# Decays of a gated delta rule read from rows spread over partitions, and formed one head pair ahead

## The reference

```python
g_f = -jnp.exp(a_log[0])[:, None] * jax.nn.softplus(a_f + dt_bias[0][:, None])
...
gc = jnp.cumsum(g.astype(f32).reshape(bn, h, n, c), axis=-1)
incl = jnp.tril(jnp.ones((c, c), dtype=bool))
strict = jnp.tril(jnp.ones((c, c), dtype=bool), -1)
decay = jnp.exp(jnp.where(incl, gc[..., :, None] - gc[..., None, :], -jnp.inf))
k_beta = k * beta
m = jnp.where(strict, jnp.einsum('bhnik,bhnjk->bhnij', k_beta, k) * decay, 0.0)
t_inv = lax.linalg.triangular_solve(eye + m, jnp.broadcast_to(eye, m.shape),
                                    left_side=True, lower=True, unit_diagonal=True)
...
intra = jnp.einsum('bhnik,bhnjk->bhnij', q, k) * decay
...
def step(s, inp):
    a_n, u_n, w_n, qd_n, kd_n, gt_n = inp
    v_new = u_n - w_n @ s
    o_n = qd_n @ s + a_n @ v_new
    s = s * gt_n + jnp.einsum('bhck,bhcv->bhkv', kd_n, v_new)
    return s, o_n
```

## Time and profile before

| | |
|---|---|
| three runs, us | 845.85, 846.38, 852.87 |
| profiled execution, us | 845.52, of it span 843.9 |
| PE busy, us | 754.1 |
| DVE busy, us | 578.0 |
| ACT busy, us | 418.9 |
| POOL busy, us | 202.4 |
| DMA moved, MB | 203.10 |
| PE granted clock over the span | 0.982 of full |
| pairs 0, 1, 2, 3 begin at, us | 90.28, 185.88, 284.76, 383.39 |

### The profile page before, as it was taken

One profiled execution on the slowest core, in us unless ns is written; L12 is line 12 of the kernel. 1 busy time (PEld: TensorE's weight loads), 2 busy tenths in 40 slices (PEclk: granted clock), 3 DMA queues, 4 the chain that ended last, 5 costly groups with the idle time before them and its releaser, 6 DMA issues.

```text
span 843.9 us, 15762 instructions
## 1 busy us (share of the span) xinstructions
PE 754.1 (89%) x6268; PEld 625.6 (74%) x6268; DVE 578.0 (68%) x861; ACT 418.9 (50%) x741; POOL 202.4 (24%) x362
## 2 busy tenths in 40 slices
PE   3998998899979998899669899989999999999974
PEld 1678887889879897799659788887777777687531
DVE  2488587768877688776876448578877775786153
ACT  3476563458434573438524335546565665573101
POOL 3102252203702344013700120011432223212201
PEclk9999999999999999999979999999999999999998
DMA  9966464666527654569866238853999999999992
GB/s 314 298 202 165 112 160 105 189 175 164 144 59 216 182 138 113 148 178 276 263 162 196 62 131 288 333 200 120 333 387 419 407 421 421 416 421 371 419 419 98
DMA packets 164678, 203.10 MB, mean 241 GB/s; under 512 B 33381, under 2 KB 137998, under 8 KB 151674
## 3 DMA queue, kind: packets, MB, share of 16 engines
q1 hardware_dynamic: 162489, 198.02, 69.4%
q0 software_dynamic: 2112, 4.04, 1.3%
HBM read 187.49 MB, written 18.10 MB: 244 GB/s over the span
## 4 chain that ended last, share of the span: by engine, by line
PE 63%; DVE 19%; DMA 10%; issue 3%; ACT 3%; POOL 1%; SPq 1%; POOLq 0%; DVEq 0%; ACTq 0%
PE bank L2558 61%; DMA raw<-in_w_e_dram 5%; DVE chan L1833 3%; DVE half_lo L1737 3%; DVE w_lo L2243 2%; PE bank L2561 2%; DMA raw<-in_w_ada_dram 1%; DMA half_raw<-in_w_out_dram 1%; SPq L622 1%; DVE lane L1913 1%; DVE lane L1942 1%; ACT w_hi L1601 1%; DMA gate_b<-dense 1%; DVE ada_sum L2063 1%; DVE ada_sum L2061 1%
## 5 line engine op out<-in xcount | busy, mean ns | idle before, releaser
L2558 PE MATMUL bank<-hT,half_hi 128*128 128x256 f32 (+1 forms) x1024 | 229.5, 319 | 10.5 <-DVE half_lo L1737 6.3
L2558 PEld LDWEIGHTS bank<-hT,half_hi 128*128 128x128 f32 x1024 | 167.5, 193 | 23.9 <-issue 9.0
L2558 PE MATMUL bank<-hT,half_lo 128*128 128x256 f32 (+1 forms) x512 | 159.9, 312 | 0.0
L1737 DVE TENSOR_TENSOR half_lo<-half_raw,half_hi 128x1024 fp32r<-128x1024 f32 x88 | 108.1, 1230 | 31.4 <-ACT half_hi L1178 30.6
L2243 DVE TENSOR_TENSOR w_lo<-raw,w_hi 128x2048 fp32r<-128x2048 f32 x36 | 88.3, 2462 | 46.5 <-ACT w_hi L1601 46.4
L2558 PE MATMUL bank<-lane 64*64 64x64 f32 (+3 forms) x1968 | 85.4, 229 | 28.3 <-DVE lane L1894 8.2
L1178 ACT CAST half_hi<-half_raw 128x1024 fp32r<-128x1024 f32 x88 | 92.0, 1048 | 32.5 <-DMA half_raw<-in_w_proj_a_dram 12.1
L2558 PEld LDWEIGHTS bank<-lane 64*64 64x64 f32 (+3 forms) x1968 | 76.5, 139 | 38.3 <-issue 21.4
L2558 PEld LDWEIGHTS bank<-hT,half_lo 128*128 128x128 f32 x512 | 98.8, 193 | 5.2
L1601 ACT CAST w_hi<-raw 128x2048 fp32r<-128x2048 f32 x36 | 68.7, 1908 | 34.2 <-PE bank L2558 18.5
L1833 DVE SCALAR_TENSOR_TENSOR chan<-bank,conv_col,chan 128x508 f32<-128x508 f32 (+3 forms) x96 | 63.2, 658 | 10.3 <-ACT chan L1249 7.7
(11 more groups left out here) (392 smaller groups left out, 1385.8 us busy)
## 6 DMA issues: line engine op xcount, KB each, us to landing
raw<-in_w_e_dram SPq DMA_DIRECT2D x96, 1024.0 KB, 10.7
half_raw<-in_w_in_dram SPq DMA_DIRECT2D x64, 512.0 KB, 4.8
half_raw<-in_w_ada_dram SPq DMA_DIRECT2D x32, 512.0 KB, 4.7
raw<-in_w_ada_dram SPq DMA_DIRECT2D x8, 1024.0 KB, 10.9
dense<-staged SPq DMA_DIRECT2D x32, 128.0 KB, 4.6
half_raw<-in_w_proj_a_dram SPq DMA_DIRECT2D x8, 512.0 KB, 5.6
half_raw<-in_w_proj_b_dram SPq DMA_DIRECT2D x8, 512.0 KB, 3.7
half_raw<-in_w_out_dram SPq DMA_DIRECT2D x8, 512.0 KB, 6.8
```

The costliest lines, as they stand in the source:

```text
L1737: dve.tensor_tensor(half_lo[m % HBUF][:, :], half_raw[n % HRING][:, :], half_hi[m % HBUF][:, :].bitcast(F32), ALU.subtract).then_inc(s["ha ...
L2558: return nc.tensor.matmul(dst, lhsT, rhs, start=start, stop=stop)
```

## The change

The cumulated decays of all heads are formed once, in `gate_totals`, as 64 rows of 128 tokens, one for each tile, head and direction. SP writes them to DRAM (`store_cum`) and reads those of one pair back, each row spread over all 128 partitions, into parts 12 to 15 of `lane` (`load_cum`, four DMAs of 256 KB). The 16 products of each pair that made the same numbers in PSUM are gone. `decay_exp` reads SBUF now and has moved: for pair 0 it stands ahead of the pairs, for pair j within the scan of pair j - 1. Freed banks let the four `scores` stand side by side in banks 4 to 7, with no wait of one for another. DVE does the four `first_level` at the start of the pair, ahead of `taps(0)`. `turn_out` waits for the `intra_mask` of the pair's tile 3, as their results share bank 7. Before, `turn_channels(0)` and `(1)` waited for `intra_mask`; now they wait for `first_level(0)` and `(1)`. The block solver on POOL and `move_inverse` on SP wait for `intra_exp` of the pair too. In `gate_sums` DVE copies the 64 rows into a `staged` buffer, and `store_cum` and `load_cum(0)` stand on SP on either side of the first `spill`. Besides, `new_value(0)` stands ahead of a cast on ACT, `ada_fold(2 * i + 1)` behind the last dense part on PE, and `ada_line_copy(2 * i + 1)` behind a copy.

```diff
         u_inv = [problems(4 + g) for g in range(4)]
-        p_blk = [problems(12 + g) for g in range(4)]
+        cum_of = [problems(12 + g) for g in range(4)]
+        p_blk = [problems(n) for n in (12, 13, 8, 9)]
 
...
 
+            def store_cum():
+                sp.wait_ge(s["gate_dve"], 4)
+                rows_of = cum_dram.rearrange("(r d n) -> r d n", d=DIRS, n=P)
+                for d in range(DIRS):
+                    load(rows_of[:, d, :], cum_rows[d * TILES * HEADS:(d + 1) * TILES * HEADS, :], s["landed_cum"])
+
+            def load_cum(p):
+                if p:
+                    sp.wait_ge(s["inverse_placed"], 4 * p)
+                else:
+                    sp.wait_ge(s["landed_cum"], 32)
+                size = 2 * DIRS * P
+                for t in range(TILES):
+                    at_ = (t * PAIRS + p) * size
+                    load(lane_part(12 + t), cum_dram[at_:at_ + size].partition_broadcast(P), s["landed_cum"])
+
             def move_rows(first, last):
...
                 spill(3 + 7 * i + 3)
+                load_cum(j)
                 after_split(DENSE_AT[3 + 7 * i + 3])
...
                 pool.wait_ge(s["m_ready"], i * TILES + TILES)
+                pool.wait_ge(s["intra_exp"], 2 * i + 2)
                 own.after(pool.memset(solved_blocks, 0.0))
...
                 act.wait_ge(s["half_used"], DENSE_AT[k] + 1)
+                if k == 2:
+                    act.wait_ge(s["landed_cum"], 32)
                 if k >= STAGES:
...
 
-            def decay_exp(g):
-                act.wait_ge(s["scores_ready"], i * 4 + (g + 1))
-                if g == 0 and i == 0:
-                    act.wait_ge(s["gate_dve"], 7)
-                cum = by_pair(bank[6 + g % 2])
+            def decay_exp(p, g):
+                if g == 0:
+                    act.wait_ge(s["landed_cum"], 32 + 64 * (p + 1))
+                    if p == 0:
+                        act.wait_ge(s["gate_dve"], 7)
                 for h in range(2):
                     for d in range(DIRS):
-                        own.mark(act.activation(p_blk[g][:, h, d, :], cum[:, h, d, :], ACT.Relu,
-                                                bias=gates[:, NEG_CUM, g, 2 * i + h, d:d + 1]))
+                        own.mark(act.activation(p_blk[g][:, h, d, :], cum_of[g][:, h, d, :], ACT.Relu,
+                                                bias=gates[:, NEG_CUM, g, 2 * p + h, d:d + 1]))
                 own.settle()
...
             def intra_exp(g):
-                cum = by_pair(bank[6 + g % 2])
+                if g == LAT:
+                    act.wait_ge(s["pair_free"], i + 1)
                 for h in range(2):
                     for d in range(DIRS):
-                        own.mark(act.activation(intra[g - LAT][:, h, d, :], cum[:, h, d, :], ACT.Relu, scale=-1.0,
+                        own.mark(act.activation(intra[g - LAT][:, h, d, :], cum_of[g][:, h, d, :], ACT.Relu, scale=-1.0,
                                                 bias=gates[:, CUM, g, 2 * i + h, d:d + 1]))
...
             ahead(DENSE_AT[2])
+            for g in range(TILES):
+                decay_exp(0, g)
             dense_copy(2)
...
                     o_scale(i - 1)
-                decay_exp(0)
+                intra_exp(2)
                 ahead(CHAN_AT[j, 0])
-                decay_exp(1)
+                intra_exp(3)
                 center(0)
...
                     o_mul(i - 1)
-                decay_exp(2)
-                decay_exp(3)
-                intra_exp(2)
                 ahead(CHAN_AT[j, 1])
                 tanh(0)
-                intra_exp(3)
                 ahead(DENSE_AT[3 + 7 * i + 0])
...
                 place_last()
+                new_value(0)
                 ahead(DENSE_AT[3 + 7 * i + 3])
-                new_value(0)
                 z_parts(0)
...
                 dense_copy(3 + 7 * i + 4)
+                decay_exp(j, 0)
+                decay_exp(j, 1)
                 state_query(2)
...
                 ahead(Z_AT[j, 1])
+                decay_exp(j, 2)
                 dense_copy(3 + 7 * i + 5)
+                decay_exp(j, 3)
                 state_query(3)
                 new_value(3)
-                ada_line_copy(2 * i + 1)
                 ahead(DENSE_AT[3 + 7 * i + 5])
                 dense_copy(3 + 7 * i + 6)
+                ada_line_copy(2 * i + 1)
                 ahead(DENSE_AT[3 + 7 * i + 6])
...
             o_scale(PAIRS - 2)
-            decay_exp(0)
-            decay_exp(1)
+            intra_exp(2)
             ahead(DENSE_AT[24])
-            decay_exp(2)
+            intra_exp(3)
             dense_copy(24)
-            decay_exp(3)
+            ahead(DENSE_AT[25])
             mix_copies()
-            ahead(DENSE_AT[25])
-            intra_exp(2)
             dense_copy(25)
-            intra_exp(3)
             dense_copy(26)
...
             def first_level(g):
+                dve.wait_ge(s["scores_ready"], i * 4 + (g + 1))
                 dve.wait_ge(s["decay_exp"], i * 4 + (g + 1))
...
                     dve.wait_ge(s["key_gates_ready"], i + 1)
-                kk = bank[4 + g % 2][:, 0:256].rearrange("p (h n) -> p h n", h=2)
+                    dve.wait_ge(s["pair_free"], i + 1)
+                kk = bank[4 + g][:, 0:256].rearrange("p (h n) -> p h n", h=2)
                 for h in range(2):
...
                 j = i + 1
-                ahead(CHAN_AT[j, 0])
                 first_level(0)
                 first_level(1)
-                taps(0)
                 first_level(2)
                 first_level(3)
+                ahead(CHAN_AT[j, 0])
+                taps(0)
                 ahead(CHAN_AT[j, 1])
...
                        gates[:, LOG_DECAY, :, :, :].rearrange("p t h d -> p (t h) d")[:, :, d])
+                for d in range(DIRS):
+                    rows_ = slice(d * TILES * HEADS, (d + 1) * TILES * HEADS)
+                    mm(bank[6][rows_, 2 * P:3 * P], gates[:, LOG_DECAY, :, :, :].rearrange("p t h d -> p (t h) d")[:, :, d],
+                       causal[:, d, :])
                 mm(bank[6][:, 64:128], ones[:, :], gates[:, LOG_DECAY, :, :, :].rearrange("p t h d -> p (t h d)"))\
...
                     pe.wait_ge(s["v_copied"], i * 2 + 2)
+                if g == LAT:
                     pe.wait_ge(s["pair_free"], i + 1)
-                if g >= 2:
-                    pe.wait_ge(s["m_ready"], i * 4 + (g - 1))
                 tok = slice(g * P, (g + 1) * P)
                 for h in range(2):
-                    mm(bank[4 + g % 2][:, h * P:(h + 1) * P], kT[i % 2][:, h, tok], kT[i % 2][:, h, tok])
+                    ins = mm(bank[4 + g][:, h * P:(h + 1) * P], kT[i % 2][:, h, tok], kT[i % 2][:, h, tok])
                     if g >= LAT:
                         q_tok = slice((g - LAT) * P, (g - LAT + 1) * P)
-                        mm(bank[4 + g % 2][:, 256 + h * P:256 + (h + 1) * P], kT[i % 2][:, h, tok], qT[i % 2][:, h, q_tok])
-                for h in range(2):
-                    for d in range(DIRS):
-                        ins = mm(by_pair(bank[6 + g % 2])[:, h, d, :],
-                                 gates[:, LOG_DECAY, g, 2 * i + h, d:d + 1].to_broadcast([P, P]), causal[:, d, :])
+                        ins = mm(bank[4 + g][:, 256 + h * P:256 + (h + 1) * P], kT[i % 2][:, h, tok], qT[i % 2][:, h, q_tok])
                 ins.then_inc(s["scores_ready"], 1)
...
                 if p < PAIRS - 1:
-                    pe.wait_ge(s["intra_exp"], p * 2 + 4)
+                    pe.wait_ge(s["intra_ready"], p * 2 + 4)
                 for h in range(2):
...
                 scores(0)
-                channels(0, 0)
                 scores(1)
-                channels(0, 1)
                 scores(2)
                 scores(3)
+                channels(0, 0)
+                channels(0, 1)
                 channels(1, 0)
...
                 solved(3)
-                ada_fold(2 * i + 1)
                 intra_sum(3)
                 dense_part(3 + 7 * i + 6, 1)
+                ada_fold(2 * i + 1)
             i = PAIRS - 1
```

20 lines of the change are left out of this document (14 added, 6 removed).

## The result

| | before | changed |
|---|---|---|
| median of the runs compared, us | 848.95 (4 runs, 845.85 to 852.87) | 863.61 (4 runs, 860.05 to 867.81) |
| profiled execution, its span | 845.52, 843.9 | 860.05, 858.4 |
| mean granted clock | 0.982 | 0.964 |
| PE busy, us | 754.1 | 752.2 |

The ratio is 1.0163, 95% interval 1.0129 to 1.0196. The forecast was 838.0, and 863.61 lies outside its range. It came out slower by over 1%, which had a chance of 0.04.

What follows compares the result with a forecast made beforehand. PE was taken to bound the kernel up to `level_p` of each pair. Terms summed to 11.45 us, less 4.5 plus 1.4 for the clock: gain 8.35, 837.2 profiled, 838.0 on the scale of the runs; range 830 to 844.

Steps and rivals of the forecast that it cites:

- that lands just in time: 0: Scans: the spread rows take 6.5 us and reach ACT when it wants them, at no cost.
- rival D: Scans: rows landing over 7 us after issue make `decay_exp` hold up `state_query(2)`; at 10.7 us, 849.1; chance 0.05.
- Numbers: Closing chances for the whole kernel: faster 0.48, within 1% 0.48, slower 0.04.
- I expect the gain to be stopped: Pairs 1 and 2: PE waits about 4.3 us at `turn_out` for `intra_mask`; removed products buy 0.1 us there.
- gains 0.1 + 2.37 = 2.45 and 0.1 + 2.01 = 2.1: Pairs 1 and 2: the inverse returns sooner, so `place_corners` no longer waits 2.37 and 2.01 us.
- -4.5 + 1.4: Granted clock: falls behind three new waits cost 4.5 us; one old fall avoided gains 1.4.
- Gain 3.5: Pair 0: PE comes 3.55 us sooner to `level_p`, where the 1.13 us wait hangs on DVE; gain 3.5.
- I take 0.3: Ahead of the pairs: added products and a DVE copy in `gate_totals` cost 0.3 us, between 0 and 1.1.
- 0.6 for pair 0 and 0.45 for pairs 1 and 2: Scans: moving `new_value(0)` ahead removes PE's 0.85 us wait, DVE late next; these gains, bounds 0 and 0.85.
- Gain 2.2: Last pair: `u_gelu` and the remainder behind it come sooner; gain 2.2 us, between 0.6 and 3.6.
- work taken from it there is time: Up to `level_p` of each pair PE works nearly without a gap, so removed work saves time until something else is late.

Runs made afterwards that it cites:

- both: Changed kernel with spread rows in their own 8 KB, loaded right behind `move_inverse`, and `intra_mask(3)` ahead of `taps(1)`: 839.58 us, ratio 0.9883.
- A quarter of the rows: Changed kernel with one spread DMA of 256 KB for each pair instead of four, other tiles' decays wrong: 848.11 us, ratio 0.9986.
- rows in a quiet place: Changed kernel with spread rows in their own 8 KB, issued right behind `move_inverse`: 852.87 us, ratio 1.0038.
- mask first: Changed kernel with `intra_mask(3)` right behind `intra_mask(2)`, ahead of `taps(1)`, in pairs 0 to 2: 849.08 us, ratio 1.0001.
- Rows of `m` first: As "both", but in pair 0 SP sends the rows of `m` ahead of the weight half: 837.86 us, ratio 0.9858.
- new value first: Kernel before the change with `new_value(0)` ahead of the cast on ACT, nothing else: 849.26 us, ratio 0.9986.

## Why the prediction was wrong

**The step that failed: "that lands just in time: 0".** The four spreads took 10.9 us in pair 1, not the 6.5 that I took. ACT then stood still for 4.68 us, and the scans lost 10.7 us where the term was 0. I had priced them by size, between a 512 KB and a 2 MB spread, and took the nearer row. Size alone does not set it. These spreads moved less than half of what weight halves moved (158 GB/s on average over 268 to 274, against 354) while the engines were just as busy, and four of 256 KB took as long as the one of 2 MB. Nor do the weight halves in flight explain more than a part: the four ahead of pair 0, issued at 75.07 with nothing still ahead of them after 75.22, took 9.5 us to land, and those in the quiet place of "both" 9.5 to 10.7. The rows differ in length (2 KB here, 4 and 16 KB in the earlier trace rows), and there are four DMAs in place of one; which of these is the reason wasn't tried. The Trainium skill (DMA: Bandwidth & Descriptors, Measured) gives 6.15 us for 1 MB, and by that figure the cost would have been 0 too; it is the span of a plain load without its issue, and the trace disagrees with 10.9 from the first issue of these spreads. "A quarter of the rows" (15.5 us back) shows that the volume is the cost, and "rows in a quiet place" (10.7 back) that the lateness is. This is rival D, as it was described, ACT's `decay_exp` in front of `state_query(2)` included. The rival's own rule, 1 us in each of three scans for each us over 7, gave 11 us at 10.7, close to what the scans lost. It was given 0.05, on the nearer of two rows. The upper bound was in the text and deserved far more. (The chances under "Numbers" also say "half of D" where 0.04 of its 0.05 went to slower.)

**"I expect the gain to be stopped" at `turn_out`.** The mechanism was right: PE stood 4.26 and 4.27 us (forecast 4.3), and DVE's L1908 ended it. That the size fits so well is in part luck, since measured from the first scores PE came 1.0 us later than walked and DVE 0.8. What failed is what came next: "gains 0.1 + 2.37 = 2.45 and 0.1 + 2.01 = 2.1". Measured from the first scores, `turn_out` stands at 21.03 us (20.17 before), and from there to `level_p` it takes 29.09 (29.10 before). POOL started 4.4 us sooner (forecast 5.4), but the images were to land 2.5 to 5 us sooner and landed 0.85 later. They wait for a weight half on SP, whose buffer is freed by DVE and ACT, and these stood still behind the `turn_out` that PE was waiting at. The prediction had the half in it, but not that its date hangs on `turn_out`. PE's wait at `level_p` fell from 3.44 to 1.89 only because PE came later too. So fronts 1 and 2 lost 0.85 and 2.05. I had costed the `turn_out` wait as a gain that stops; "mask first" shows that it is worth 14.5 us.

**The clock, "-4.5 + 1.4".** It fell behind each of the new waits, as forecast (0.57 at 212 to 216, 0.50 at 316 to 320 and at 408 to 412), and also at a place I had not named, 243 to 247. The Trainium skill (TensorE: Matmul & The Clock Gate, HAM oscillation) warns of such falls behind waits, and the trace agrees with it behind these three. But the price that shows is small: with the clock held at 1.00 behind `turn_out` the median was 1.8 us lower, against the 3 I had counted for the two, and even that is inside the noise. Nor does the mean clock order the kernels: the profiled executions of "mask first" and of the changed kernel both have 0.964, at 852.78 and 860.05 us.

**Pair 0, "Gain 3.5".** It was 2.09, and in the two other traces of the same calls 0.9 and 0.7. `level_p` is waited for 2.64 us there, not 1.13. SP sent the rows of `m` beside a weight half: 8.4 us from the stores to the load of the blocks, 5.1 before. "Rows of `m` first" bears this out in part: with the rows sent alone front 0 was 1.8 us shorter, but `level_p` still waited 2.90.

**Ahead of the pairs, "I take 0.3", bounds 0 and 1.1.** It was 2.60. What I had left out is a queue: `load_cum(0)` stands ahead of weight halves on SP, and ACT's cast waits 3.61 us for its half at 86.77. That half took 9.9 us to land.
```profile
86.77 1.05 ACT L1202 CAST half_hi<-half_raw 128x1024 fp32r<-128x1024 f32 x1 [3.61 <-DMA half_raw<-in_w_in_dram]
```
The size of that transfer is what costs. "A quarter of the rows" has 92.95 us there too, but its whole start came 2.9 us late. Measured from SP's issue of the weight half ahead of the first spill, pair 0 begins 19.47 us later in the kernel before and 19.47 in "a quarter of the rows", 22.33 in the changed kernel, and 19.97 to 22.42 in the nine others with four spreads. ACT waits 2.8 to 3.7 us for a half in all ten of these, and in no trace without them. So the term was 2.9 us in the profiled execution and 0.5 to 3.0 over all ten, 0.8 in the middle one. The rest of the differences in this column is when SP reached that first half: 70.54 to 73.83 us, whatever the kernel.

**Scan, "0.6 for pair 0 and 0.45 for pairs 1 and 2".** Not borne out: in the trace of "new value first" DVE is late next by 0.84 us, which the text had named as the lower bound, though the runs cannot tell 1.5 us from none.

**Last pair, "Gain 2.2".** It was -0.30. `turn_mix` waited 4.38 us (forecast 4.2 to 4.8). `u_gelu` came in time, as forecast: ACT's wait of 2.98 us for it is gone. But PE's two waits for remainders fell only from 5.6 to 4.8 us in all, and the mean clock of the stretch was 0.86, against 0.90 before.

**"work taken from it there is time".** This reading of the page, the first step of all, holds only with a condition. In the kernel before, 8 us of products less gave nothing that shows: fronts 1 and 2 are closed by the inverse, for which `level_p` still waited 3.35 us in pair 1. In "both" the same kind of work costs its full length. A PE that is 89% busy had hidden the second limit.

## What to carry to other kernels

Price a new DMA by a row of its own kind, not by its size alone, and count what stands behind it in the queue as well. When the bounds are 4 us apart beside a tight wait, let the far one carry real chance. Before counting removed work as gained, ask which date closes the stage, and whether a queue in order ties that date to the engine that you freed. When an addition costs more than it saves, test the placement of its parts before giving it up: here one moved line, and one load moved into 8 KB of its own, turned +1.6% into -1.2%.

## What was not expected of the hardware

- A spread of 2 KB rows over 128 partitions kept the DMA engines at 0.97 to 1.02 busy and moved 132 to 192 GB/s, against 354 for weight halves; in a quiet place four took 9.5 to 10.7 us. One of 256 KB for a pair landed in 5.0 us (median, "a quarter of the rows"); four took 10.9.
- ACT is no faster from SBUF than from PSUM for these tiles: a Relu of 128x128 took 399 ns from the spread rows, 367 from PSUM in the kernel before.
```profile
L1327 ACT ACTIVATE lane<-lane,gates 128x128 f32<-128x128 f32 x64 | 20.5, 399 | 11.6 <-DMA lane<-cumulated 11.6
```
- The granted clock of 0.57 behind a wait of 4.3 us did not come when 36 idle products of 128x128 filled it.
